# A two-layer encoder on one core: the softmax divisions taken off GpSimd, top-k cut into parts, and a new order at the seams between stages

## The reference

```python
h = rms_norm(x, norm_mix[layer])
(aq, ak, av, bq, bk, bv, iq, ik, iw, cq, ckv, kr, gate_logits) = split(h @ w_in[layer])
o_a = window attention with sinks (8 heads, 64 wide)
o_b = sparse attention: an indexer scores the keys, each query keeps 64, softmax over those
o_c = latent attention: cq, ckv normalised, times w_uq and w_ukv, rotary keys, softmax
merged = sum over a, b, c of sigmoid(gate) * (o @ w_branch)
x = x + merged @ w_out[layer]
x = x + cross_attention(rms_norm(x), rms_norm(mem), xa_wq, xa_wkv, xa_wo)
x = x + (swiglu(rms_norm(x)) on layer 0, the top 2 of 8 experts on layer 1)
```

## Time and profile before

| what | value |
|---|---|
| median of 3 runs | 2062.62 us |
| the profiled execution's own time | 2064.47 us |
| its span | 2062.7 us |
| TensorE, mean granted clock | 0.986 |
| VectorE busy | 1553.6 us |
| ScalarE busy | 1291.3 us |
| GpSimd busy | 110.0 us |
| start to the first layer's dense mixer | 0 to 400 us |
| dense mixer | 400 to 641 us |
| second layer to its experts | 641 to 1045 us |
| experts and the last norm | 1045 us to the end |

### The profile page before, as it was taken

The page is one execution under the profiler, slowest core; times in us unless marked ns, Lnnn a source line. Parts: engine busy times, 40 slices in busy tenths (PEclk is TensorE's granted clock), DMA queues, the critical chain, the costliest instruction groups (busy, mean ns, idle before and its releaser), DMA issues.

```text
span 2062.7 us, 28183 instructions
## 1 busy us (share of the span) xinstructions
PE 1968.2 (95%) x9434; PEld 1618.3 (78%) x9434; DVE 1553.6 (75%) x1753; ACT 1291.3 (63%) x1663; POOL 110.0 (5%) x98
## 2 busy tenths in 40 slices
PE   6998999999998988999889999999999999999998
PEld 5876778788887876778768888888888888888886
DVE  4776675554555776675579899898989989899897
ACT  3545654444443544654368787887778878778785
POOL 1131100000000131100000000000000000000000
PEclk9999999999999999999989999999999999999999
DMA  8342554455553342454359999999999999999994
GB/s 269 122 173 83 184 195 142 140 205 182 200 178 129 112 164 102 166 192 156 120 203 373 342 360 366 331 363 331 367 356 346 369 328 365 352 355 367 328 371 161
DMA packets 227907, 513.04 MB, mean 249 GB/s; under 512 B 8208, under 2 KB 19280, under 8 KB 227840
## 3 DMA queue, kind: packets, MB, share of 16 engines
q1 hardware_dynamic: 223584, 502.51, 68.2%
q0 software_dynamic: 2160, 7.52, 1.2%
q10 hardware_dynamic: 2096, 2.12, 0.3%
HBM read 511.05 MB, written 1.07 MB: 248 GB/s over the span
## 4 chain that ended last, share of the span: by engine, by line
PE 88%; DVE 4%; ACT 3%; issue 2%; DMA 2%; POOL 0%; SPq 0%; DVEq 0%; ACTq 0%; POOLq 0%
PE bank L824 15%; PE bank L830 15%; PE bank L825 15%; PE bank L1604 7%; PE bank L1610 7%; PE bank L1618 7%; PE bank L641 4%; PE bank L651 4%; PE bank L647 4%; PE bank L1631 2%; DVE wlo L470 2%; PE bank L776 2%; PE bank L792 2%; ACT whi L467 1%; PE bank L1653 1%
## 5 line engine op out<-in xcount | busy, mean ns | idle before, releaser
L470 DVE TENSOR_TENSOR wlo<-raw,whi 128x1024 fp32r<-128x1024 f32 (+3 forms) x958 | 1152.5, 1238 | 249.1 <-ACT whi L467 227.8
L467 ACT ACTIVATE whi<-raw 128x1024 fp32r<-128x1024 f32 (+3 forms) x958 | 995.5, 1056 | 292.8 <-PE bank L830 148.6
L824 PE MATMUL bank<-whi,xg_hi 128*128 128x512 f32 x896 | 354.5, 396 | 1.8 <-ACT whi L467 1.8
L825 PE MATMUL bank<-whi,xg_lo 128*128 128x512 f32 x896 | 349.2, 390 | 0.0
L830 PE MATMUL bank<-wlo,xg_hi 128*128 128x512 f32 x896 | 276.5, 390 | 0.0
L830 PEld LDWEIGHTS bank<-wlo,xg_hi 128*128 128x128 f32 x896 | 168.1, 188 | 36.3 <-DVE wlo L470 0.5
L824 PEld LDWEIGHTS bank<-whi,xg_hi 128*128 128x128 f32 x896 | 168.3, 188 | 36.0 <-ACT whi L467 2.6
L825 PEld LDWEIGHTS bank<-whi,xg_lo 128*128 128x128 f32 x896 | 168.4, 188 | 33.3
L1604 PE MATMUL bank<-whi,hT_hi 128*128 128x512 f32 (+3 forms) x576 | 154.4, 392 | 26.8 <-DVE merged L2081 16.8
L824 PE MATMUL bank<-whi,hidT_hi 128*128 128x512 f32 x448 | 175.1, 391 | 0.0
L825 PE MATMUL bank<-whi,hidT_lo 128*128 128x512 f32 x448 | 174.4, 389 | 0.0
(11 more groups left out here) (309 smaller groups left out, 2137.1 us busy)
## 6 DMA issues: line engine op xcount, KB each, us to landing
raw<-in_moe_w_gu SPq DMA_DIRECT2D x224, 1024.0 KB, 5.6
raw<-in_moe_w_down SPq DMA_DIRECT2D x112, 1024.0 KB, 5.6
raw<-in_w_in SPq DMA_DIRECT2D x34, 1024.0 KB, 4.9
raw<-in_ffn_w_gu SPq DMA_DIRECT2D x28, 1024.0 KB, 5.0
raw<-in_xa_wkv SPq DMA_DIRECT2D x16, 1024.0 KB, 5.1
raw<-in_ffn_w_down SPq DMA_DIRECT2D x14, 1024.0 KB, 4.8
raw<-in_w_branch SPq DMA_DIRECT2D x12, 1024.0 KB, 4.9
raw<-in_w_out SPq DMA_DIRECT2D x8, 1024.0 KB, 5.0
```

The lines of the kernel that those rows point to most:

```text
L467: self.eng.activation(whi[:, ps, 0:size], src, ACT.Copy).then_inc(high_ready, mark(high_ready, "high", p))
L470: self.eng.tensor_tensor(wlo[:, ps, 0:size], src, whi[:, ps, 0:size].bitcast(F32), ALU.subtract).then_inc(low_ready, mark(low_ready, "low" ...
L824: pe.matmul(o, hi[:, k], wh, start=first and (c == 0 or outs[0] != outs[1]), stop=False)
L825: pe.matmul(o, lo[:, k], wh, start=False, stop=False)
```

## The change

Eight things are edited; the semaphores that go with them are left out below.

1. The first loads. SyncE loads the identity, the first half of x's columns, the first gain, the second half of x, waits for the first half, loads the first weight unit, the remaining constants, and the other units. ScalarE loads the two tables. PE takes piece 0 of PA between the halves of T1; ScalarE's and VectorE's sequences follow. The turning of the bias rows moves behind PB's first piece.
2. The division: VectorE multiplies heads 0 to 3, ScalarE heads 4 to 7, in A, B and C. GpSimd has neither these nor B's mask, which VectorE adds.
3. `topk` takes a range of rounds; they are spread over other places.
4. index_scores(1) moves behind GA's first pieces; splits in GB, YB and GC are called at other places, and C's first softmax feeds YB.
5. In cross attention, `weigh_x(., 1)` moves ahead of XO's second piece.
6. T3's first half is taken out of its banks before XO is finished.
7. The dense mixer's first group takes gate's and up's pieces of the first half of h, then those of the second.
8. The dense mixer's last down product is cut by columns rather than by rows; the first half of the columns is added to x, multiplied by the next gain and turned while the second is computed. The second layer's T1 is in two halves like the first's.

```diff
@@ dense_pe @@
-            def gate_up(g, p, between=None):
+            def gate_up_first(g, p):
+                for b0, reader in ((0, "act"), (2, "dve")):
+                    for t in range(NT):
+                        fill(pe, b0 + t, reader)
+                for n_, (b0, i) in enumerate(((0, 0), (0, 1), (2, 0), (2, 1), (0, 2), (0, 3), (2, 2), (2, 3))):
+                    if n_ == 2:
+                        turn_rest()
+                    columns(p + n_, b0, i, None if b0 else i // 2)
+                    if i == 3:
+                        same(g, "GU"[b0 // 2])
...
+            def down_last(g, p):
+                for c in range(2):
+                    for n_ in range(2):
+                        if c and n_:
+                            turn_next()
+                        piece(p + 2 * c + n_, [(hidT_hi[:, t, 2 * n_ + k], hidT_lo[:, t, 2 * n_ + k], k, 4 + 2 * t + c, False, n_ == 1 and k == 1)
+                                               for k in range(2) for t in range(NT)], None, None if c or n_ else g)
+                    same("dense", "out", c)
@@ SyncE @@
-            sp.dma_start(onehot_sb[:, :], onehot).then_inc(table_loaded, mark(table_loaded, "onehot", by=16))
...
+            sp.dma_start(ident, consts[:, C_IDENT:C_IDENT + P]).then_inc(ident_loaded, mark(ident_loaded, "ident", by=16))
+            sp.dma_start(x[:, :, 0:512], x_in[:, :, 0:512]).then_inc(x_loaded[0], mark(x_loaded[0], "x_in", 0, by=16))
+            sp.dma_start(gain[0][:, :], a["norm_mix"][0].partition_broadcast(P)).then_inc(
+                first_gain_loaded, mark(first_gain_loaded, 0, "mix", "gain", by=16))
+            sp.dma_start(x[:, :, 512:1024], x_in[:, :, 512:1024]).then_inc(x_loaded[1], mark(x_loaded[1], "x_in", 1, by=16))
+            sp.wait_ge(x_loaded[0], at("x_in", 0))
@@ ScalarE @@
+            def normalise(l, m, t, buf):
+                st = sstats[:, MIX[m], t]
+                act.wait_ge(inverse_ready, at(l, m, "inverse", t))
+                for hh in range(4, 8):
+                    act.activation(buf[:, hh, 0:NK[t]], buf[:, hh, 0:NK[t]], ACT.Copy, scale=st[:, 3, hh:hh + 1]).then_inc(
+                        probs_by_act, mark(probs_by_act, l, m, "P by act", t))
...
-                if l == 0:
-                    act.wait_ge(x_loaded, at("x_in"))
-                else:
-                    act.wait_ge(x_settled, at("x_moved", l - 1, 1))
-                sp_.through(l, "PA", 0)
-                to_high(l, "T1", hT_hi)
-                norm_sums(l, "mix", x, merged)
+                sp_.upto(l, "PA", 0, -1)
+                to_high(l, "T1", hT_hi, (0,))
+                sp_.upto(l, "PA", 0, 0)
+                to_high(l, "T1", hT_hi, (1,))
...
                 softmax(l, "A", 1, 8, S, smA[1], True)
+                normalise(l, "A", 0, smA[0])
...
                 sp_.upto(l, "GB", 0, 2)
+                normalise(l, "B", 0, smB[0])
                 softmax(l, "B", 1, 8, S, smB[1], name="GB")
                 sp_.upto(l, "GB", 1, 0)
                 probs_out(l, "B", 0)
+                normalise(l, "B", 1, smB[1])
                 gates(l, "GB", 0)
...
-                softmax(l, "C", 0, 8, P, smC[0])
+                softmax(l, "C", 0, 8, P, smC[0], name="YB")
...
-                act.wait_ge(piece_used, at("lin", l, "XO", 1, 1))
-                to_high(l, "T3", hT_hi, (0,))
+                act.wait_ge(piece_used, at("used", blocks[(l, "XO", 1)].piece0 + 1))
+                to_high(l, "T3", hT_hi, (0,))
@@ TensorE @@
-                turn_all(l, "T1", h, norm_ready, lambda q, t: (l, "mix", "h", q, t))
-                linear(l, "PA", 0, hT_hi, hT_lo, "T1")
+                if l == 0:
+                    turn_all(l, "T1", h, norm_ready, lambda q, t: (l, "mix", "h", q, t), (0,))
+                linear(l, "PA", 0, hT_hi, hT_lo, "T1", last=1)
+                turn_all(l, "T1", h, norm_ready, lambda q, t: (l, "mix", "h", q, t), (1,))
+                linear(l, "PA", 0, hT_hi, hT_lo, "T1", first=1)
...
+                pe.wait_ge(rope_step, at(l, "qrope1", "done"))
...
-                linear(l, "XO", 0, hT_hi, hT_lo, "X", "pv", last=2)
+                linear(l, "XO", 0, hT_hi, hT_lo, "X", "pv", last=1)
                 weigh_x(0, 1)
                 weigh_x(1, 1)
@@ VectorE @@
+            def normalise(l, m, t, buf):
+                inverse(l, m, t, 8, m == "A")
+                v = buf[:, 0:4, 0:NK[t]]
+                dve.wait_ge(inverse_ready, at(l, m, "inverse", t))
+                dve.tensor_tensor(v, v, sstats[:, MIX[m], t, 3, 0:4].unsqueeze(2).to_broadcast([P, 4, NK[t]]), ALU.mult).then_inc(
+                    probs_by_dve, mark(probs_by_dve, l, m, "P by dve", t))
+            def add_mask(l, t):
+                v = smB[t][:, :, 0:NK[t]]
+                dve.tensor_tensor(v, v, score[:, t, 0:NK[t]].unsqueeze(1).to_broadcast([P, 8, NK[t]]), ALU.add).then_inc(
+                    masked, mark(masked, l, "masked", t))
...
                 sp_.upto(l, "UQ", 0, 0)
-                topk(l, 0, "UKV", 0, 0)
-                sp_.upto(l, "UKV", 0, 0)
+                topk(l, 1, 0, 4)
+                sp_.upto(l, "UQ", 0, 1)
                 for b in range(2):
                     evac(l, "UQ", b, 1, lambda bb: [(uq_dst(1, b), bb[:, 0:512 - 256 * b], 1.0)])
+                    sp_.upto(l, "UKV", 0, b - 1)
                 sp_.upto(l, "YA", 0, 0)
+                topk(l, 1, 4, 6)
                 for b in range(2):
                     evac(l, "UKV", b, 1, lambda bb: ukv(bb, 1, b))
+                    if b == 0:
+                        topk(l, 1, 6, 8)
...
                 scaled_scores(l, "B", 1, pair_banks(1), smB[1], biasB, HD ** -0.5)
-                topk(l, 1, "GB", 0, 0)
                 for t in range(NT):
                     merge(l, "YA", 0, t, True)
+                sp_.upto(l, "GB", 0, -1)
                 take_out(l, "TK", TK(l))
                 sp_.upto(l, "GB", 0, 0)
-                dve.wait_ge(masked, at(l, "masked", 0))
+                add_mask(l, 0)
                 masked_max(l, "B", 0, 8, P, smB[0])
...
                 sp_.upto(l, "GB", 0, 2)
-                dve.wait_ge(masked, at(l, "masked", 1))
+                add_mask(l, 1)
+                normalise(l, "B", 0, smB[0])
                 masked_max(l, "B", 1, 8, S, smB[1])
-                inverse(l, "B", 0, 8)
                 scaled_scores(l, "C", 0, line_banks(0), smC[0], None, C_QK ** -0.5)
...
+                to_low(l, "T3", hT_hi, hT_lo, (0,))
                 add_to_x(l, "XO", 1, 0)
-                to_low(l, "T3", hT_hi, hT_lo, (0,))
...
                     dense_dve(dve, sp_)
+                    dense_out(dve, 0)
+                    dve.wait_ge(gain_loaded[0], at(1, "mix", "gain"))
+                    for t in range(NT):
+                        times_gain(1, "mix", 0, t)
```

More of the change, by code:

```diff
@@ L418, in trunk @@
         vector_step = sem("vector_step")
-        x_loaded = sem("x_loaded")
-        x_settled = sem("x_settled")
+        x_loaded = [sem(f"x{q}_loaded") for q in range(2)]
+        ident_loaded = sem("ident_loaded")
+        first_gain_loaded = sem("first_gain_loaded")
         y_normed = sem("y_normed")
@@ L664, in gate_up, with down @@
                     for i in range(4):
-                        if g == "dense first" and b0 == 0 and i == 2:
-                            turn_rest()
-                        columns(p + 2 * b0, b0, i, 0 if g == "dense first" and b0 == 0 else None)
-                        if b0 and i == 1 and between:
+                        columns(p + 2 * b0 + i, b0, i)
+                        if b0 and i == 1:
                             turn_hidden(g, between)
                     same(g, "GU"[b0 // 2])
-            def down(g, p, last):
-                for t in range(NT):
-                    pe.wait_ge(dve_freed[t], at("lo", g, "hid", t))
+            def down(g, p):
                 for i in range(4):
-                    piece(p + i, [(hidT_hi[:, t, i], hidT_lo[:, t, i], c, 4 + 2 * t + c, False, last and i == 3)
-                                  for c in range(2) for t in range(NT)])
-            gate_up("dense first", P0)
+                    piece(p + i, [(hidT_hi[:, t, i], hidT_lo[:, t, i], c, 4 + 2 * t + c, False, False)
+                                  for c in range(2) for t in range(NT)], None, None if i else g)
+            def down_last(g, p):
[6 more added lines that the diff above has]
+                    same("dense", "out", c)
+            gate_up_first("dense first", P0)
             pe.wait_ge(expert_step, at("dense", "zero"))
@@ L686, in dense_pe @@
                 gate_up("dense", P0 + 8, [previous("dense", "act", t) for t in range(NT)])
-                down("dense", P0 + 16, False)
+                down("dense", P0 + 16)
             turn_hidden("dense last", [final("dense", "act", t) for t in range(NT)])
-            down("dense last", P0 + PIECES - 4, True)
-            same("dense", "out")
+            down_last("dense last", P0 + PIECES - 4)
```

(13 more changed lines are left out.)

145 lines of the change are left out of this document (80 added, 65 removed).

## The result

The changed kernel takes **2026.86 us** (median of 4 runs, 2026.09 to 2028.15) against 2062.57 of the kernel before on the same chip: a ratio of 0.9823, 95% interval 0.9810 to 0.9836. The forecast was 2017.0 with a range of 2004 to 2033: the direction is right and the range holds it, but 9.9 us of the gain are missing. It lies just above the 2008 to 2026 that the forecast called its own, and inside the range only by the half that was taken in of the rival "VectorE becomes the bound", which isn't what happened. The profiled execution took 2026.83 (span 2025.0), 37.6 us less than the one of before; the sum had promised 45.8.

What follows compares the result with a forecast made beforehand. TensorE, busy 95% of the span, was the bound; only gaps and half clock could be won. 2.5 + 31.2 + 3.2 + 1.2 - 2.8 + 10.5 = 45.8 off 2064.5 gives 2018.7, as a median 2017; range 2004 to 2033.

Steps and rivals of the forecast that it cites:

- the 2008 to 2026: Whole kernel: the forecast's own range without the rivals, given a chance of 0.48.
- VectorE becomes the bound: Rival, mixers: 9.3 us come at VectorE's densest, double stalls with half clock cost 12 more, start 3.4: 2032, chance 0.18.
- The start: First loads: first matmul near 16.5, 4.5 us earlier, but bias rows issued later, landing near 40: +2.5 us.
- an idle stretch: Sign of being wrong: TensorE idle for several microseconds at the bias rows.
- late bias rows: Rival, start: load keeps its 21.4 us from a later issue, TensorE stands 5.7 us: -0.9 for +2.5, 2020, chance 0.12.
- The mixers: Each layer: 21.6 us of TensorE's waits removed, 6.0 of new waits and half clock: 15.6, for both layers 31.2.
- New waits in GB: Mixers, each layer: 3 us before C's second scores, 1.1 for TQ, others, less today's stalls 4.7, half clock 1.3: 6.0.
- A's mixer: At the first wlo wait, index_scores moves behind a split, but the next piece waits for ScalarE: 0.6 us counted.
- Off GpSimd: Mixers, each layer: masks and multiplications leave GpSimd, adding 9.3 us to VectorE and 8.6 to ScalarE.
- Cross attention and the dense end: Cross attention: waits covered, 3.2 and 1.2 us. Dense mixer's end: half the columns finished earlier, 10.5 us, bounds 5 and 11.5.
- The dense start: Dense mixer's start: bank claims 0.6, Silu wait 2.6, less 0.4 of launch: -2.8 us, bounds -3.2 and -1.
- Slower, and nothing: Rivals: added VectorE and ScalarE work lies on GB's path, 2086, chance 0.03; nothing measurable, chance 0.02.

Runs made afterwards that it cites:

- bias_mid: Changed kernel with ScalarE issuing the load of the bias rows ahead of the second half's bank copies instead of behind them: 2017.68 us.
- dense_start: `silu`'s edit on the changed kernel, plus up's banks claimed only before the third piece, third and fourth pieces split before T3's second half: 2018.46 us.
- bias_first: Changed kernel with the bias rows' load issued ahead of everything else ScalarE does in the first layer, once the bias vector is stored: 2019.75 us.
- ga_order: Changed kernel; ScalarE splits GA's third and fourth piece before the latent norm's squares, VectorE splits and copies before the first four top-k rounds: 2022.30 us.
- on_pool: Changed kernel with mask and division back on GpSimd, top-k rounds still spread: 2034.10 us.
- both_back: Changed kernel with the top-k rounds in one stretch each again and mask and division back on GpSimd: 2048.11 us.
- combo2: Changed kernel with `bias_mid`, `dense_start` and `ga_order`, plus C's scores taken out earlier and high parts made earlier in GB: 1998.64 us.
- silu: Changed kernel with ScalarE splitting the first dense block's seventh and eighth piece before its two Silu instead of behind them: 2025.19 us.

## Why the prediction was right, and where it wasn't

- **The bound and the direction**: right. TensorE's gaps and its half clock were what could be won, and the expert loop's time didn't change: of the 37.6 us, 37.7 were there at its start.
- **The start** is the first step that failed: +2.5 predicted, -0.2 measured. The first matmul at 14.53 was better than the 16.5 forecast, and that gain was lost at the bias rows, where the prediction's own sign of being wrong, an idle stretch, came up with 3.5 us. The issue was seen (21.2 measured, 22 said). The load was to land at 40.0 and landed at 41.3: it took 20.0 us, neither the 18 of the sum nor the 21.4 of the earlier trace rows, which the rival "late bias rows" kept. So this rival happened in part, with 3.5 of its 5.7 us of waiting. 1.3 of the missing 2.7 us are this later landing. The rest is a term that the prediction left out: the products behind the wait ran at half clock, and from their start to TA it took 8.5 us instead of the 6.6 of before (0.5 of this came back in the piece that moved ahead of them). In all nine traces with a wait of 3.5 to 3.8 us there, the 16 products take 8.6 to 9.9 us; in the four without a wait, 7.03. `bias_mid` shows both: the same load, issued 8 us sooner, takes 19.8, and 6.4 us come back. That the result is nearer to the rival's -0.9 than to +2.5 is partly luck, since the rival had no half clock either. The rule weighed there, of the Trainium skill (DMA: Bandwidth & Descriptors, Queues, rings and completion order), gave -0.9 by keeping the 21.4. No run shows the load alone; beside the weights it took 18.9 to 21.4 us in all fourteen traces, wherever it was issued from 11.7 on.
- **The mixers**: 15.6 predicted, 13.5 and 12.4 measured. Most of the difference is half clock: 3.4 us a layer in this execution, of which the prediction counted 1.3. In the traces of `dense_start` and `bias_first`, whose mixers are the same and ran without any, the gain is 15.9 and 14.9. Removed up to the turns of TQ: 17.9 said (6.5 and 11.4), 16.8 and 16.0 measured. The attribution was half wrong: the 8.4 us were put down to the second tile's rounds alone, and 3.8 of them were a split between the rounds that waited for ScalarE. The sum was unhurt, since the change moves both. New waits in GB: 6.0 said, 5.4 measured (1.2 for qCT, 1.1 said; 2.1 for smC, 3 said; the second scores of C in 5.38 us, of which some 1.7 are half clock). Before GC and YB 3.1 said, 2.5 measured.
- **A's mixer**: 0.6 predicted, -0.4 and -0.6 measured. The prediction named the cause (the next piece waits for ScalarE, which waits for the copy behind `index_scores`) and priced it too low: 2.9 us, and in this execution 1.7 of half clock. In `dense_start` and `bias_first`, where no half clock followed, the same stretch is 1.1 and 0.8 us shorter than before. `ga_order` takes the wait away.
- **Off GpSimd** is the first thing that the title names, and with the rounds spread it is worth 1.5 us (traces) to 3.3 us (medians) of a layer's 13. The prediction gave it no sum of its own, so it couldn't be right or wrong. What it adds was priced well: ScalarE is busy for 8.3 us more a layer (1291.3 to 1307.8 in both), 8.6 said, although the terms given, 3 x (1.2 + 1.6), make 8.4.
- **VectorE as the bound**, the rival with 0.18: no, none of the double stalls that it asks for is there. VectorE's busy time fell from 1553.6 to 1551.8 although it took over 9.3 us a layer by the prediction's estimate. The reason is in its splits. Groups by form, VectorE, 90 to 250 us (busy us, mean ns), first in the changed kernel, then in `on_pool`:

```profile
L473 DVE TENSOR_TENSOR wlo<-raw,whi 128x1024 fp32r<-128x1024 f32 x42 | 51.1, 1230 | 20.6 <-ACT whi L470 20.3
```

```profile
L473 DVE TENSOR_TENSOR wlo<-raw,whi 128x1024 fp32r<-128x1024 f32 x41 | 63.0, 1551 | 17.7 <-ACT whi L470 17.4
```

  12 us a layer more for the same splits where GpSimd works beside them. What the Trainium skill says (SBUF — State Buffer, SBUF: two separate sides): a VectorE operation with both inputs in SBUF and a GpSimd operation that reads SBUF hold one pair of ports in turn, each for a whole instruction. The traces agree: 1.23 us a split on the mean in the changed kernel; in `both_back` two splits together take 4.54 beside GpSimd's mask (148.16 to 151.48), which is one of 1.2 and one that ends 1.1 us after the mask; and in `on_pool` a single split beside the second tile's mask (151.33 to 155.91) takes 4.60 and again ends 1.1 us after it. The rows of `both_back` and of `on_pool`:

```profile
148.03 4.54 DVE L473 TENSOR_TENSOR wlo<-raw,whi 128x1024 fp32r<-128x1024 f32 x2
```

```profile
152.40 4.60 DVE L473 TENSOR_TENSOR wlo<-raw,whi 128x1024 fp32r<-128x1024 f32 x1
```
- **Cross attention and the dense end**: right. 2.0 for 1.6, 3.2 for 2.8, 10.3 for 10.5. The turns and PA's first piece stand under the additions as it was said, and PA's second block starts 11.7 us after the dense mixer's last matmul (12 said).
- **The dense start**: right in mechanism, all three waits where they were named, -3.6 for -2.8: the claimed banks cost 2.3 us, 1.0 more than the wait of before, where 0.6 had been counted; the Silu's wait was 2.3 for 2.6; and the 0.4 "of launch" that the sum takes off is a term that no run shows: the waits alone grew by 3.35.
- **Slower, and nothing**: no sign of either.

## What to carry to other kernels

Before a wait is put down to the work ahead of it on its engine, read the idle time inside that work: one split that waits for another engine's part can be half of it. Where several engines follow hand-written orders, a call that waits for another engine should stand behind everything that others already wait for, and the part it needs should be made in the other engine's idle stretch; such moves at six places were worth 28 us here, several times the change's step off GpSimd. When a wait is forecast, say what it costs if the work behind it runs at half clock: at the bias rows that was more than the error in the load's own time. And before a difference of a few microseconds between two traces is put down to an edit, take the half clock off both: here it moved the same code by 4 us.

## What the runs showed that was not expected

**The same stall is followed by half clock in one execution and not in another.** After a wait of 2.12 us the second scores of C took 5.38 us in the changed kernel; after 2.11 us in `dense_start`, in the same place, 3.69:

```profile
169.80 3.69 PE L1688 MATMUL bank<-kCT,qCT 96*128 96x256 f32 x16 [2.11 <-DVE smC L2063]
```

The windows of the two kernels over these products (us, TensorE's busy time and count, weight loads, VectorE, ScalarE, GpSimd, granted clock, DMA share, GB/s):

```profile
170.47:175.50 5.03, 5.03 (x16) 4.14 (x17) 3.55 (x6) 5.03 (x16) 0.00 (x0) 0.66 0.00 0
```

```profile
169.80:173.50 3.70, 3.70 (x17) 3.29 (x18) 2.22 (x4) 3.70 (x14) 0.00 (x0) 1.00 0.00 0
```

The level is 1.2 GHz for most of the first, 2.4 for the second. For a layer's mixers this makes anything from 191.0 to 195.2 us with one and the same code. At waits of 2 to 3 us it looks like chance: the 2.9 us wait for `whi` in GA stands twice in each of eight traces, and half clock followed it 8 times of 16. Added up as above, half clock cost 17.6 us in the profiled execution of before, 12.1 in that of the changed kernel, 6.6 in `dense_start`, 3.5 in `combo2`. Executions of one kernel differ in it: `bias_mid` ran in 2015.8 us at a mean clock of 0.995 and in 2020.8 at 0.992. That spread is larger than `silu`'s whole effect of 2.3 us. A term for half clock behind a stall of 2 to 3 us is therefore a chance of 1.7 us, not a sum. Whether a spread between executions comes from this alone isn't shown: `combo2`, with the stalls gone, spreads over 1.5 us, but `both_back`, which has most of them, over 0.9.
